# Attention scores and the V product as pairs of half-array matmuls in a fused encoder layer

## The reference

```python
sc = jnp.einsum("bqkgd,bskd->bkgqs", q_blk, k)      # q already times 64 ** -0.5
pr = jax.nn.softmax(sc, axis=-1)
return jnp.einsum("bkgqs,bskd->bqkgd", pr, v)       # k: 2 kv heads, g: 4 query heads each
```

## Time and profile before

| what | value |
|---|---|
| median of three runs | 1227.14 us |
| runs | 1227.68, 1225.36, 1227.14 us |
| profiled execution, first to last instruction | 1227.0 us |
| PE busy | 1125.2 us, 92% |
| DVE busy | 850.3 us, 69% |
| ACT busy | 602.9 us, 49% |
| GpSimd busy | 364.2 us, 30% |
| mean granted TensorE clock | 0.965 of 2.4 GHz |
| attention and SSD loop | about 237 to 401 us of the span |

### The profile page before, as it was taken

How to read it: one execution, slowest core, us unless ns; L and a number is a source line. 1 busy time by engine, 2 the same in 40 slices (tenths; PEclk the granted TensorE clock), 3 DMA queues, 4 the chain that set the end, 5 groups by cost and what they waited for, 6 DMA issues and landing times.

```text
span 1227.0 us, 13573 instructions
## 1 busy us (share of the span) xinstructions
PE 1125.2 (92%) x4706; PEld 736.3 (60%) x4706; DVE 850.3 (69%) x1026; ACT 602.9 (49%) x741; POOL 364.2 (30%) x275
## 2 busy tenths in 40 slices
PE   5999869789998999999999999999999999999950
PEld 3568758565665454344466777777777777777630
DVE  5436783557778154273358888988888889988738
ACT  1143244456575110110256676687666776787522
POOL 0007992244544000000100333322333333322313
PEclk9999889979999999999999999999999999999985
DMA  9010100300000930200559999999999999999815
GB/s 331 6 69 4 66 1 1 103 1 1 1 1 2 317 136 35 94 26 26 175 214 332 384 382 389 390 379 390 384 395 381 385 389 395 382 386 380 311 29 202
DMA packets 74886, 253.86 MB, mean 207 GB/s; under 512 B 7384, under 2 KB 9304, under 8 KB 74848
## 3 DMA queue, kind: packets, MB, share of 16 engines
q1 hardware_dynamic: 69440, 234.49, 50.1%
q0 software_dynamic: 5408, 18.88, 5.7%
HBM read 237.62 MB, written 15.73 MB: 206 GB/s over the span
## 4 chain that ended last, share of the span: by engine, by line
PE 80%; DVE 9%; POOL 5%; issue 2%; ACT 2%; DMA 1%; SPq 0%; ACTq 0%; DVEq 0%; POOLq 0%
PE ps L1880 15%; PE ps L1882 14%; PE ps L1881 14%; PE ps L1792 7%; PE ps L1760 7%; PE ps L1558 4%; PE ps L1664 2%; PE ps L1679 2%; PE ps L1552 2%; PE ps L1861 2%; PE ps L1797 2%; DVE xT L1451 1%; DVE ring L1206 1%; PE ps L1790 1%; PE ps L1655 1%
## 5 line engine op out<-in xcount | busy, mean ns | idle before, releaser
L1327 DVE TENSOR_TENSOR low<-late,high 128x2048 fp32r<-128x2048 f32 x192 | 427.1, 2283 | 31.5 <-ACT high L698 31.5
L698 ACT ACTIVATE high<-late 128x2048 fp32r<-128x2048 f32 x192 | 354.9, 1914 | 24.0 <-DMA late<-in_w_e_up 23.7
L661 POOL COPY idx_now<-idxT 96x1 int32 (+1 forms) x30 | 132.7, 4423 | 375.3 <-DVE xa L1368 203.2
L1880 PE MATMUL ps<-high,xeT 128*96 128x512 f32 x528 | 210.8, 399 | 6.8 <-issue 4.8
L1882 PE MATMUL ps<-high,xeT 128*96 128x512 f32 x528 | 208.9, 396 | 0.0
L1881 PE MATMUL ps<-low,xeT 128*96 128x512 f32 x528 | 208.4, 395 | 0.0
L1880 PEld LDWEIGHTS ps<-high,xeT 128*96 128x96 f32 x528 | 86.0, 163 | 43.3 <-issue 6.1
L1882 PEld LDWEIGHTS ps<-high,xeT 128*96 128x96 f32 x528 | 85.9, 163 | 37.7 <-issue 0.5
L1881 PEld LDWEIGHTS ps<-low,xeT 128*96 128x96 f32 x528 | 86.0, 163 | 36.3 <-issue 0.3
L1880 PE MATMUL ps<-high,hidT 128*96 128x512 f32 x240 | 95.5, 398 | 2.3 <-DVE low L1327 2.3
L1882 PE MATMUL ps<-high,hidT 128*96 128x512 f32 x240 | 94.2, 393 | 0.0
(11 more groups left out here) (255 smaller groups left out, 1858.1 us busy)
## 6 DMA issues: line engine op xcount, KB each, us to landing
late<-in_w_e_gate SPq DMA_DIRECT2D x64, 1024.0 KB, 6.9
late<-in_w_e_up SPq DMA_DIRECT2D x64, 1024.0 KB, 8.0
late<-in_w_e_down SPq DMA_DIRECT2D x64, 1024.0 KB, 8.1
ring<-in_w_in SPq DMA_DIRECT2D x3, 2048.0 KB, 9.1
ring<-in_w_ple_gate SPq DMA_DIRECT2D x2, 2048.0 KB, 11.5
ring<-in_w_in SPq DMA_DIRECT2D x3, 1024.0 KB, 13.0
x_rows<-xa POOLq DMA_DIRECT2D x6, 512.0 KB, 2.9
acc_rows<-mix POOLq DMA_DIRECT2D x12, 256.0 KB, 2.3
```

The costliest lines, as they stand in the source:

```text
L661: return nc.gpsimd.tensor_copy(idx_now[:, col:col + 1], idxT[:, bass.ds(e, 1)])
L698: return nc.scalar.activation(o, i, ACT.Copy)
L1327: nc.vector.tensor_tensor(low[j], raw[j], high[j], ALU.subtract).then_inc(s_low, 1)
L1880: nc.tensor.matmul(o, lhs[0][:, k, :], high[j][:, c], start=(k == 0), stop=False)
```

## The change

Scores use 64 rows of the array: the query head's 64 rows against the 64 rows of the unpadded keys `kT`. The units of a tile are ordered by pair, so that the heads of kv head 0 and 1 alternate, and PE issues the two scores of a pair together in every even step. The V product is done once per tile, after eight units, as pairs of matmuls with 64 weight columns each, whose results go to the lower and the upper 64 rows of one PSUM bank; one copy then takes all 128 rows. `kz`, its clearing on GpSimd and one of the two key copies per tile on ScalarE go. A third `probT` buffer is added. The factor 64 ** -0.5 moves into the query norm weights (one small GpSimd operation), and the maximum is negated in the reduction itself, so L1175 goes.

```diff
-        kz = xT[:, 4:6, :]
+        kT = xT[:, 4, :]
-        probT = [xrows[:, 0:2048].rearrange("p (b c) -> p b c", b=4),
+        probT = [xT[:, 5:8, :].rearrange("p k c -> p (k c)")[:, 0:2048].rearrange("p (b c) -> p b c", b=4),
+                 xrows[:, 0:2048].rearrange("p (b c) -> p b c", b=4),
...
-        att_units = [(t, 4 * i + j) for t in range(NT) for i in range(NKV) for j in range(4)]
+        att_units = [(t, 4 * i + j) for t in range(NT) for j in range(4) for i in range(NKV)]
+        UPT = NQ
...
+            pool.wait_ge(s_param, 16 * 9)
+            nc.gpsimd.tensor_scalar(qkw[:, 0, :], qkw[:, 0, :], HD ** -0.5, None, ALU.mult).then_inc(s_qs, 1)
             pool.wait_ge(s_xa, NT)
+            pool.wait_ge(s_qs, 1)
...
-                if n == len(upd) // 2 + 2:
-                    pool.wait_ge(s_proj, len(groups))
-                    nc.gpsimd.memset(kz, 0.0).then_inc(s_kz, 1)
...
-            act.wait_ge(s_kz, 1)
+            act.wait_ge(s_proj, len(groups))
...
-                for i in range(NKV):
-                    last = copy(kz[i * HD:(i + 1) * HD, i, tc], ps[i * HD:(i + 1) * HD, b + 1, 0:P])
-                last.then_inc(s_qkT, 1)
+                copy(kT[:, tc], ps[:, b + 1, 0:P]).then_inc(s_qkT, 1)
...
-                                     bias=att[:, 0, u:u + 1], scale=HD ** -0.5,
+                                     bias=att[:, 0, u:u + 1],
...
-                ch.link(nc.vector.reduce_max(att[:, 2, u:u + 1], ps[:, u % 3, 0:L], X))
-                nc.vector.tensor_scalar(att[:, 0, u:u + 1], att[:, 2, u:u + 1], -(HD ** -0.5), None,
-                                        ALU.mult).then_inc(s_max, 1)
+                nc.vector.tensor_reduce(att[:, 0, u:u + 1], ps[:, u % 3, 0:L], X, ALU.max,
+                                        negate=True).then_inc(s_max, 1)
...
-            def att_out(G):
-                t, i = G // NKV, G % NKV
-                dve.wait_ge(s_pv, G + 1)
-                nc.vector.tensor_copy(mix[i * HD:(i + 1) * HD, t, 0:512],
-                                      ps[i * HD:(i + 1) * HD, 4, :]).then_inc(s_ao, 1)
+            def att_out(t):
+                dve.wait_ge(s_pv, t + 1)
+                nc.vector.tensor_copy(mix[:, t, 0:512], ps[:, 4, :]).then_inc(s_ao, 1)
...
-                if i % 4 == 0 and i >= 8:
-                    att_out(i // 4 - 2)
+                if i >= 12 and (i - 12) % UPT == 0:
+                    att_out((i - 12) // UPT)
...
-                nc.tensor.matmul(ps[:, u % 3, 0:n * P], qT[:, h % 4, t * P:(t + 1) * P],
-                                 kz[:, h // 4, a * P:(a + n) * P], start=True, stop=True).then_inc(s_sc, 1)
+                r = slice(h // 4 * HD, (h // 4 + 1) * HD)
+                nc.tensor.matmul(ps[:, u % 3, 0:n * P], qT[r, h % 4, t * P:(t + 1) * P],
+                                 kT[r, a * P:(a + n) * P], start=True, stop=True).then_inc(s_sc, 1)
...
-            def pv(G):
-                a, n = seq_of[G // NKV]
-                pe.wait_ge(s_pts, 4 * G + 4)
-                if G:
-                    pe.wait_ge(s_ao, G)
+            def pv(t):
+                a, n = seq_of[t]
+                pe.wait_ge(s_pts, UPT * (t + 1))
+                if t:
+                    pe.wait_ge(s_ao, t)
                 for b in range(n):
-                    last = nc.tensor.matmul(ps[:, 4, :], kvd[:, a + b, P:2 * P], probT[G % 2][:, b, :],
-                                            start=(b == 0), stop=(b == n - 1))
+                    for i in range(NKV):
+                        last = nc.tensor.matmul(ps[i * HD:(i + 1) * HD, 4, :],
+                                                kvd[:, a + b, P + i * HD:P + (i + 1) * HD],
+                                                probT[(2 * t + i) % 3][:, b, :], start=(b == 0), stop=(b == n - 1))
                 last.then_inc(s_pv, 1)
...
-                if i < NU:
+                if i < NU and i % 2 == 0:
                     scores(i)
+                    scores(i + 1)
...
-                if i >= 7 and i % 4 == 3:
-                    pv((i - 7) // 4)
+                if i >= 11 and (i - 11) % UPT == 0:
+                    pv((i - 11) // UPT)
```

More of the change, by code:

```diff
@@ L242, in hymba_layer @@
         s_rope = sem("s_rope")
-        s_kz = sem("s_kz")
+        s_qs = sem("s_qs")
         s_tap = sem("s_tap")
@@ L483, in _ @@
             sp.dma_start(bB[:], bc(A["ln1_b"][0])).then_inc(s_ln1, 16)
-            sp.wait_ge(s_ao, NG)
+            sp.wait_ge(s_ao, NT)
             sp.wait_ge(s_yo, NG)
@@ L1180, in pt_out @@
                 dve.wait_ge(s_pt, u + 1)
-                if u >= 8:
-                    dve.wait_ge(s_pv, u // 4 - 1)
-                nc.vector.tensor_copy(probT[u // 4 % 2][:, 0:n, (u % 4) * P:(u % 4 + 1) * P],
-                                      ps[:, 3, 0:n * P].rearrange("p (b c) -> p b c", c=P)).then_inc(s_pts, 1)
-            def att_out(G):
-                t, i = G // NKV, G % NKV
-                dve.wait_ge(s_pv, G + 1)
-                nc.vector.tensor_copy(mix[i * HD:(i + 1) * HD, t, 0:512],
-                                      ps[i * HD:(i + 1) * HD, 4, :]).then_inc(s_ao, 1)
+                t, h = att_units[u]
+                b = 2 * t + h // 4
+                if b >= 3:
+                    dve.wait_ge(s_pv, (b - 3) // 2 + 1)
+                nc.vector.tensor_copy(probT[b % 3][:, 0:n, (h % 4) * P:(h % 4 + 1) * P],
+                                      ps[:, 3, 0:n * P].rearrange("p (b c) -> p b c", c=P)).then_inc(s_pts, 1)
+            def att_out(t):
+                dve.wait_ge(s_pv, t + 1)
+                nc.vector.tensor_copy(mix[:, t, 0:512], ps[:, 4, :]).then_inc(s_ao, 1)
             def weights(n):
@@ L1802, in _ @@
             mix_turn(3)
-            pe.wait_ge(s_ao, NG)
+            pe.wait_ge(s_ao, NT)
             pe.wait_ge(s_yo, NG)
```

## The result

The changed kernel has a median of 1240.93 us over four runs (1236.42 to 1241.31); the kernel before, measured beside it, 1227.41 (1225.36 to 1227.68). The ratio is 1.0106, its 95% interval 1.0089 to 1.0124. The forecast was 1227.

What follows compares the result with a forecast made beforehand. The SSD circle (11.5 us) and PE's own order (13.8) were taken to bound the loop's groups by turns. Terms -5.4 + 3.8 + 1.1 + 0.6 - 1.0 = -0.9, plus 0.9 of clock, made 1227 us; range 1219 to 1244.

Steps and rivals of the forecast that it cites:

- clock term: In the loop: emptier PE brings two more short falls of the granted clock, +0.9 us, bounds 0 to +8.
- the rival in which V does not overlap: Scores overlap, V products do not: 3.0 us more in three groups and the end, 1241 us; chance 0.08 with its reverse.
- groups 5, 7, 9 (no V product): Sample groups left without a V product: period 11.98 us, 1.79 less than 13.77, three times, -5.4 us.
- groups 6, 8, 10 (with V product): Sample groups that do a whole tile's V product: period 15.05 us, 1.28 more, three times, +3.8 us.
- What bounds the kernel: Loop: the SSD's circle needs some 11.5 us per group; PE's own order makes it 13.8 with long V products.
- The price of a pair: Paired half-array matmuls on PE: half overlap, 1.29 us per score pair and 3.86 for a tile's V product.
- The rival of full overlap: Pairs on PE cost 0.86 us and V 3.43; groups 11.55 without V, 13.76 with; 1220.6 us, chance 0.25.
- The clock rival: The clock stays low through about four prompt or sample groups, 2.0 us each: 1234 us, chance 0.08.
- Boundaries: Each change of matmul shape on PE costs about 0.19 us, zero where PE waits anyway.
- The lump: V work of two groups put into one, with `y` waiting behind it: periods alternate between about 12 and 15 us.
- Before the loop: Clearing `kz` and the second key copy go from the chain: between 0 and 1.9 us saved, taken as -1.0.
- The new waits: Early scores waiting for an earlier exponential, and the third buffer's waits on V products already issued: nothing.

Runs made afterwards that it cites:

- experiment 7: The kernel before plus unread matmuls in the gaps of its first five groups only: 1224.52 us, ratio 0.9977.
- experiment 1: The changed kernel plus unread full-array matmuls ahead of transposes in odd steps, ahead of `y` in groups without V product, and behind the last unit: 1216.84 us.
- experiment 9: The changed kernel, V product every four units in two pieces, unread matmuls in remaining gaps: 1211.38 us; two more ahead of `y` in groups 1 to 3: 1209.67.
- experiment 3: The changed kernel with the V product issued for the whole first kv head, then the second: 1240.84 us, ratio 1.011.
- experiment 5: The kernel before, nothing paired or moved: with 64-row scores 1235.76 us; in a second run with 64-column V products 1228.76 us.
- experiment 6: The kernel before with only the first half of each V product's matmuls, the rest of the sum left out: 1215.98 us, ratio 0.991.
- experiment 4: The changed kernel with the V product issued one whole kv head after the other and a pair's scores issued in separate steps: 1254.23 us.
- experiment 2: The changed kernel plus unread matmuls, in two runs: only ahead of `y` 1217.85 us; only ahead of every second transpose 1227.33 us.
- experiment 8: The changed kernel with the V product every four units on half the columns, both kv heads in pairs, nothing unread added: 1215.61 us.

## Why the prediction was wrong

It named both mechanisms and gave each the wrong size, in opposite directions. The pairs were priced too dear: without its clock term the forecast changes the loop by -0.9 us, and at full clock it changed by -10.3, of which about 2.4 is low clock that the kernel before had lost (experiment 7), so the change by itself was worth some -8. The clock was priced too cheap: +0.9 us, against some +20, the rest of the way to the +11.8 measured. The measured time lies inside the stated range of 1219 to 1244 us by luck, since the range was built on the price of overlap; and the 1241 us of the rival in which V does not overlap is met by luck too, since V overlaps fully.

The table sets its terms beside the same groups of the profiled runs, as differences to before in us. The periods between decay ends were, for groups 0 to 10, 13.06 (13.02 in the earlier trace rows, whose window starts 0.04 us later), 10.85, 11.05, 11.50, 11.51, 13.44, 13.62, 13.88, 13.61, 14.04 and 14.01 before, 13.07, 13.82, 12.65, 11.96, 12.11, 13.96, 15.94, 13.18, 17.85, 13.47 and 15.84 after, and 10.60, 10.59, 10.58, 10.85, 10.81, 11.81, 13.71, 11.83, 13.70, 11.82 and 13.59 in experiment 1.

| term | forecast | after | full clock (experiment 1) |
|---|---|---|---|
| groups 5, 7, 9 (no V product) | -5.4 | -0.7 | -5.9 |
| groups 6, 8, 10 (with V product) | +3.8 | +8.4 | -0.2 |
| groups 2 and 4 | +1.1 | +2.2 | -1.2 |
| groups 0, 1 and 3 | 0 | +3.4 | -3.4 |
| up to the first decay's end | -1.0 | -1.6 | -1.1 |
| from the last decay to `out_proj` | +0.6 | +0.1 | +1.5, with its fillers |
| sum | -0.9, and +0.9 of clock | +11.8 | -10.3 |

- **What bounds the kernel** held. The loss, and the gain of experiment 1, lie before `out_proj` to within 0.5 us; the floor of 11.5 us that the circle allows was reached in experiment 9 (11.55).
- **The price of a pair failed**: "records go in program order, so the order is A, A, B, B, and only the second of A can run beside the first of B" gave 1.29 and 3.86. The trace shows 0.86 plus 0.2 of boundary for the scores (1.06 from 327.68 to 328.74), and 3.59 with its boundary for V. Experiment 3 shows why: a record of one half passes waiting ones of the other. The rule of the Trainium skill that stood behind the rival (TensorE: Matmul & The Clock Gate, Part 3: Packing small matmuls) is the one that the trace agrees with: the Trainium skill has starts about 4 ns apart, this trace 0.01 us (324.09 and 324.10).
- **The rival of full overlap** was right in its periods: 11.55 and 13.76 against 11.8 and 13.7. Its 1220.6 us would have been 1219.7 without the 0.9 for the clock; experiment 1 is 1216.8, with 3.4 gained in the prompt's groups 0, 1 and 3 that the rival did not count. The changed kernel came out 20 us above this rival because the rival had the forecast's clock term.
- **The clock term failed**: "I take two more short falls, +0.9; the bounds are none and four whole groups, 0 to +8". Low clock was in all eleven groups and is worth 24.1 us by the medians of the changed kernel and experiment 1, of which the kernel before had lost about 2.4 too (experiment 7). Two things were missed. The gap ahead of `y` was in the forecast's own sum: the groups without a V product have PE done at +8.37 and `y` at +9.09, a gap of 0.7, and 1.2 with full overlap; the earlier trace rows show that such stillness had come before both falls. And the price of a low group was too small: a transpose step takes 1.09 instead of 0.63, so `y` and the decay end later, and everything behind them starts late. The price of 2.0 us came from one prompt group, which at a mean clock of 0.65 was low for only some 9 of its 13 us and in which PE has slack, and not from a sample group with a V product, where 15.8 to 17.9 us stand against 13.7.
- **The clock rival** (1234 us, chance 0.08) had the right mechanism and a third of the size.
- **Boundaries** were sized right, 0.19 where they are on the path (experiment 5).
- **The lump** was right in direction: at full clock, groups with a V product last 1.9 us longer than those without (forecast 3.1). What was not seen is that the emptied group is where the harm is done.
- **Before the loop**: -1.6 against -1.0, but the gain is not shown. Kernels whose program up to there does not differ end the first decay at 237.30 (experiment 6) to 239.79 us (experiment 5, columns) with the old keys and at 236.22 (experiment 3) to 238.61 (experiments 1 and 4) with the new, so one pair of executions cannot resolve 1 us. What the trace does show is that clearing `kz` is gone from the chain of waits, which now goes through DVE's state updates:

```profile
229.23 0.76 DVE ring L1167
...
235.50 0.70 PE ps L1641 x4
236.20 1.95 PE ps L1681 x16
```

- **The new waits**, priced at nothing, held: between 285 and 392 us PE waited for GpSimd's sum and for the copies ahead of the transposes, and for nothing else.

Left open: what exactly decides whether a gap is followed by a fall, and how long the fall lasts. Gaps of 1.34 us were followed by falls in the changed kernel and not in the last groups of experiment 3, and those of 1.65 in the prompt of experiment 6 cost little. Full-array fillers elsewhere shortened the falls (experiment 2), while in experiment 4 a PE without an idle moment stayed at 1.2 GHz for 13.7 us. The runs show that filling the gap ahead of `y`, or spreading the V product so that it does not open, is enough in the sample groups, and no more than that.

## What to carry to other kernels

Work taken off TensorE can cost more than it saves when the engine is then busy unevenly: look for the gap that it opens ahead of a step that waits for another engine (here 1.3 to 1.8 us), and read the granted clock there before trusting a sum of durations. Where a tuned loop is near one bound, spread the work that is left rather than lump it (experiment 8: 25 us, most of it clock, for halving the lump), and to find out what the clock costs, add unread matmuls in the gaps: if the time falls and the granted clock rises, the clock was the loss. Price a low clock from the fullest group that it can reach.

## What was not expected of the hardware

- Adding 108 MATMUL records (4814 against 4706) made the kernel 24 us faster.
- Records for the two halves of the array are not held to program order: with eight of one half issued ahead of eight of the other, the second half started after four slots (353.90 against 352.12 us).
- A pair of 32-bit half-array matmuls, two records each, takes hardly longer than one full matmul: eight of 512 columns in 3.59 us with a boundary, where four took 3.43.
- A gap of 1.77 us ahead of `y`, in a loop where PE is otherwise busy most of the time, was followed by 10.2 us at half clock (from 311.1 to 321.3 us).
- A fall can outlast steady work: with 64-row scores and no idle moment on PE, the clock stayed at 1.2 GHz from 321.7 to 335.4 us (experiment 4).
